# Joining setup, first feed-forward half and RWKV mixing into one block of a two-layer decoder kernel

## What is computed

```python
def rmsnorm(x, g):
    return x * lax.rsqrt(jnp.mean(x * x, axis=-1, keepdims=True) + NORM_EPS) * g

def swiglu(x, w_gate, w_up, w_down):
    return (jax.nn.silu(x @ w_gate) * (x @ w_up)) @ w_down

x = x + 0.5 * swiglu(rmsnorm(x, norm_ffn1[0]), ...)        # D_FF = 2816
# rwkv7_time_mix of h = rmsnorm(x, norm_mix[0]):
xx = jnp.pad(h, ((0, 0), (1, 0), (0, 0)))[:, :-1] - h      # the token before, minus this one
x_r, x_w, x_k, x_v, x_a, x_g = [h + xx * mu[i] for i in range(6)]
r, k, v = x_r @ W_r, x_k @ W_k, x_v @ W_v                  # 1024 x 1024 each
lw = tanh(x_w @ w_lora_a)                                  # 1024 x 64
la = x_a @ a_lora_a                                        # 1024 x 64
lg = sigmoid(x_g @ g_lora_a)                               # 1024 x 160
```

## Time and profile before

| what | value |
|---|---|
| median of three runs | 2573.34 us |
| profiled execution | 2577.01 us |
| its span | 2575.2 us |
| PE busy | 2364.7 us, 92% |
| DVE busy | 1577.5 us, 61% |
| ACT busy | 621.9 us, 24% |
| POOL busy | 576.6 us, 22% |
| mean granted PE clock | 0.96 |
| PE idle before its matmuls of `mix_project` | 28.7 us |

### The profile page before, as it was taken

The page is one execution under the profiler, slowest core; times in us unless marked ns, Lnnn a source line. Parts: engine busy times, 40 slices in busy tenths (PEclk is TensorE's granted clock), DMA queues, the critical chain, the costliest instruction groups (busy, mean ns, idle before and its releaser), DMA issues. The chain is left out here.

```text
span 2575.2 us, 44022 instructions
## 1 busy us (share of the span) xinstructions
PE 2364.7 (92%) x17558; PEld 1920.7 (75%) x17558; DVE 1577.5 (61%) x2151; ACT 621.9 (24%) x1211; POOL 576.6 (22%) x382
## 2 busy tenths in 40 slices
PE   5999995996889869999999999999949998999999
PEld 4888883774666747888888788888738887788887
DVE  5656467982777745656576565657636666565654
ACT  3101012222555432100022310101525552110001
POOL 2202034431222122212130120203221201221211
PEclk8999996998999979999999999999969899999999
DMA  4333321342110022333346233333351102233332
GB/s 119 96 99 98 98 76 54 115 121 84 33 32 26 11 58 86 102 88 102 88 140 184 80 94 95 97 92 103 92 126 38 39 1 66 82 106 90 102 89 71
DMA packets 377090, 217.21 MB, mean 84 GB/s; under 512 B 18881, under 2 KB 360833, under 8 KB 376929
## 3 DMA queue, kind: packets, MB, share of 16 engines
q1 hardware_dynamic: 368800, 199.09, 27.5%
q10 hardware_dynamic: 8128, 15.83, 1.8%
HBM read 199.00 MB, written 15.89 MB: 83 GB/s over the span
## 5 line engine op out<-in xcount | busy, mean ns | idle before, releaser
L150 PE MATMUL bank_b<-hhi_b,w_hi_b 128*128 128x512 f32 x872 | 346.6, 398 | 3.1 <-DVEq L314 3.1
L152 PE MATMUL bank_b<-hhi_b,w_lo_b 128*128 128x512 f32 x872 | 340.9, 391 | 0.0
L151 PE MATMUL bank_b<-hlo_b,w_hi_b 128*128 128x512 f32 x872 | 340.9, 391 | 0.0
L143 DVE TENSOR_TENSOR w_lo_b<-w_raw,w_hi_b 128x1024 fp32r<-128x1024 f32 (+1 forms) x165 | 289.7, 1756 | 5.7
L150 PEld LDWEIGHTS bank_b<-hhi_b,w_hi_b 128*128 128x128 f32 x872 | 164.7, 189 | 40.9 <-DVEq L314 3.8
L151 PEld LDWEIGHTS bank_b<-hlo_b,w_hi_b 128*128 128x128 f32 x872 | 164.7, 189 | 36.7 <-issue 2.9
L152 PEld LDWEIGHTS bank_b<-hhi_b,w_lo_b 128*128 128x128 f32 x872 | 164.6, 189 | 34.6
L446 POOL TENSOR_TENSOR act_b<-gated_b,usc_b 128x512 f32<-128x512 f32 x44 | 63.9, 1452 | 487.9 <-ACT gated_b L423 487.9
L150 PE MATMUL bank_a<-hhi_a,w_hi_a 128*128 128x512 f32 x352 | 138.5, 393 | 17.5 <-DVE w_lo_a L143 11.9
L332 DVE TENSOR_TENSOR gsc_b<-bank_b,rstd_b 128x512 f32<-128x512 f32 x44 | 30.4, 692 | 194.5 <-PE bank_b L152 184.1
L423 ACT ACTIVATE gated_b<-gsc_b 128x512 f32<-128x512 f32 x44 | 27.9, 634 | 494.8 <-DVE gsc_b L332 494.8
(11 more groups left out here) (366 smaller groups left out, 5204.2 us busy)
## 6 DMA issues: line engine op xcount, KB each, us to landing
w_raw<-in_ffn_w_gate_dram SPq DMA_DIRECT2D x88, 512.0 KB, 3.8
w_raw<-in_ffn_w_up_dram SPq DMA_DIRECT2D x88, 512.0 KB, 3.9
w_raw<-in_ffn_w_down_dram SPq DMA_DIRECT2D x64, 512.0 KB, 3.8
w_raw<-in_ffn_w_down_dram SPq DMA_DIRECT2D x32, 384.0 KB, 3.3
w_raw<-in_rw_w_rkv_dram SPq DMA_DIRECT2D x24, 512.0 KB, 4.2
rkv_scratch<-staged_mix ACTq DMA_DIRECT2D x24, 256.0 KB, 2.4
w_raw<-in_kv_w_dram SPq DMA_DIRECT2D x12, 512.0 KB, 4.9
w_raw<-in_rw_w_o_dram SPq DMA_DIRECT2D x8, 512.0 KB, 4.8
```

Source lines behind the costliest of these rows:

```text
L143: nc.vector.tensor_tensor(lo, raw, fp(hi), ALU.subtract).then_inc(s["w_ready"], 1)
L150: nc.tensor.matmul(out, whi, hi, start=first, stop=False)
L151: nc.tensor.matmul(out, whi, lo, start=False, stop=False)
L152: return nc.tensor.matmul(out, wlo, hi, start=False, stop=last)
```

## The change

Setup, the first Ffn and the mixing become one Block with one Region, one weight ring and one set of semaphores.

- **Entry** takes the place of `setup`. PE transposes the vectors first, then x. DVE, not ACT, copies the x tiles from PSUM, two of them ahead of the splits of units 0 and 1, and the other six between the low parts of the Ffn's first norm. Units 2 and 3 are split after the low parts.
- **Mix** takes the place of `mix_project`. A mixed tile is now h(shifted) * mu + h * (1 - mu): ACT makes the second product (`part_tile`), DVE multiplies and adds the first (`mixed_tile`), ACT rounds, and DVE makes the low part (`low_tile`), which POOL did. POOL has nothing to do in Mix. The table 1 - mu (`one_mu`) is made once by DVE.
- The factor of the norm is exp(-0.5 ln(ms)), two ACT operations, in place of ACT's root and DVE's reciprocal.
- The first three r units run side by side, tile by tile; before it was one.
- The mixing's first four units are loaded and split by the ring at the end of the Ffn. On DVE each unit is now: mix and lower the tiles beside it, then split the unit four ahead.
- r and v tiles use the Ffn's `hhi` and `hlo`, k tiles its `ahi` and `alo`; only lw, la and lg use a pair allocated behind `h`. The four slots of unfinished tiles and the two of outputs are in the Ffn's `gsc`, `usc`, `gated` and `act32`.

```diff
@@ class Ffn: vector, scalar, gpsimd @@
-        if self.first:
-            region.split(dve, 0)
-            for d in range(ND):
-                self.norm.vector_tile(dve, d)
-            for u in range(1, 4):
-                region.split(dve, u)
@@ class Mix (new, in place of mix_project) @@
+    def mixed_tile(self, dve, m):
+        d = self.tiles[m][1]
+        dve.wait_ge(self.s["tmp"], m + 1)
+        at = self.core.row["rw_mu"] + self.column(m)
+        self.core.nc.vector.scalar_tensor_tensor(out=self.slot(m), in0=self.h[:, d, 0:T], scalar=self.core.vecs[:, at:at + 1], in1=self.slot(m),
+                                                 op0=ALU.mult, op1=ALU.add).then_inc(self.s["mix32"], 1)
+    def low_tile(self, dve, m):
+        name, d = self.tiles[m]
+        hi, lo = self.pair[name]
+        dve.wait_ge(self.s["mix_hi"], m + 1)
+        self.core.nc.vector.tensor_tensor(lo[:, d], self.slot(m), fp(hi[:, d]), ALU.subtract).then_inc(self.s["mix_lo"], 1)
+    def vector(self, dve):
...
+        self.normal_tile(dve, 0)
+        self.normal_tile(dve, 1)
+        for d in range(ND):
+            self.mixed_tile(dve, d)
+            if d + 2 < ND:
+                self.normal_tile(dve, d + 2)
+            if d:
+                self.low_tile(dve, d - 1)
+        self.low_tile(dve, ND - 1)
+        for u in range(len(self.units)):
+            made = self.made_beside(u)
+            for m in made:
+                self.mixed_tile(dve, m)
+            for m in made:
+                self.low_tile(dve, m)
+            self.region.split(dve, self.base + u + 4)
+    def part_tile(self, act, m):
+        s, (_, d) = self.s, self.tiles[m]
+        act.wait_ge(s["h"], d + 1)
+        if m >= 4:
+            act.wait_ge(s["mix_lo"], m - 3)
+        self.core.nc.scalar.activation(self.slot(m), self.h[:, d, 1:T + 1], ACT.Copy,
+                                       scale=self.one_mu[:, self.column(m):self.column(m) + 1]).then_inc(s["tmp"], 1)
+    def scalar(self, act):
...
+        A(region.ms[:], region.bank[:, 6], ACT.Ln, scale=1.0 / D, bias=self.core.eps[:, 0:1]).then_inc(s["ln"], 1)
+        act.wait_ge(s["ln"], 1)
+        A(region.rstd[:], region.ms[:], ACT.Exp, scale=-0.5).then_inc(s["rstd"], 1)
+        self.part_tile(act, 0)
+        for d in range(ND):
+            if d + 1 < ND:
+                self.part_tile(act, d + 1)
+            self.high_tile(act, d)
+        for u, (name, j) in enumerate(self.units):
+            made = self.made_beside(u)
+            for m in made:
+                self.part_tile(act, m)
+            for m in made:
+                self.high_tile(act, m)
+            act.wait_ge(region.ring["w_free"], done(self.base + u))
...
+    def tensor(self, pe):
+        s, region = self.s, self.region
+        self.norm.tensor_sum(pe)
+        for k in range(ND):
+            pe.wait_ge(s["mix_lo"], k + 1)
+            for u in range(3):
...
+                mm = three_passes(self.core, region.bank[:, u], u, k, hi[:, k], lo[:, k], k == 0, k == ND - 1)
@@ class Entry (new, in place of setup) @@
+    def vector(self, dve, norm):
...
+        residual(0)
+        residual(1)
+        self.region.split(dve, 0)
+        self.region.split(dve, 1)
+        dve.wait_ge(s["vecs"], 2)
+        for d in range(ND):
+            if d + 2 < ND:
+                residual(d + 2)
+            dve.wait_ge(s["copied"], d + 1)
+            norm.vector_tile(dve, d)
+        self.region.split(dve, 2)
+        self.region.split(dve, 3)
+        r = core.row["rw_mu"]
+        V.tensor_scalar(self.one_mu[:], core.vecs[:, r:r + 6 * ND], -1.0, 1.0, ALU.mult, ALU.add)
+    def tensor(self, pe):
...
+        pe.wait_ge(s["rows"], 16 * self.loads)
+        for tile, n in enumerate((P, core.rows - P)):
+            mm = core.nc.tensor.transpose(bank[:, tile, 0:n], self.rows[0:n, tile], core.ident[0:n, 0:n])
+        mm.then_inc(s["rows_turned"], 1)
+        pe.wait_ge(s["x"], 16 * NT)
+        for d in range(ND):
+            if d >= 4:
+                pe.wait_ge(s["copied"], d - 3)
...
@@ opening @@
+        region = Region(core, ctx, tag, early=[sb("tok", [P, NT, D]), sb("rows", [P, 2, P])])
+        h = region.sb("h", [P, ND, T + 1])
+        extra = region.sb("mhi", [P, ND, T], F32R), region.sb("mlo", [P, ND, T], F32R)
...
+            entry.vector(dve, ffn.norm)
             ffn.vector(dve)
+            mix.vector(dve)
```

More of the change, by code:

```diff
@@ L159, with __init__ @@
 class Region:
-    def __init__(self, core, ctx, tag, wide=(), narrow=()):
+    def __init__(self, core, ctx, tag, wide=(), narrow=(), early=()):
         self.core, self.nc, self.ctx, self.tag = core, core.nc, ctx, tag
-        self.owned, self.units = {}, []
+        self.owned, self.units, self.right = {}, [], set()
+        self.early = self.alias(*early)
         self.wide = [self.alias(*rows) for rows in wide]
@@ L197, in take, with cols @@
         return base
+    def cols(self, u):
+        m = self.units[u].shape[2]
+        return slice(P - m, P) if u in self.right else slice(0, m)
     def load(self, sp, u):
         if u >= SLOTS:
-            load_unit(sp, self.ring, self.core, u % SLOTS, u, self.units[u])
+            load_unit(sp, self.ring, self.core, u % SLOTS, u, self.units[u], self.cols(u))
     def split(self, dve, u):
@@ L205, in split @@
             _, k, m = self.units[u].shape
[L206 removed]
+            split_unit(dve, self.ring, self.core, u % SLOTS, u // SLOTS, u, k, m, self.cols(u))
 class Norm:
@@ L411, in scalar @@
         act.sem_inc(s["silu"], 1)
-        if self.first:
-            for d in range(ND):
-                self.norm.scalar_tile(act, d)
         self.norm.scalar_root(act)
@@ L434, in gpsimd @@
         pool.sem_inc(s["a_lo"], 1)
-        if self.first:
-            for d in range(ND):
-                self.norm.pool_tile(pool, d)
         ftile = 0
@@ L1997, in opening @@
+def opening(core, weights, tag, gain, rkv, lora, ahead):
+    with ExitStack() as ctx:
+        sb = lambda name, shape, dt=F32: (f"{name}", shape, dt)
+        region = Region(core, ctx, tag, early=[sb("tok", [P, NT, D]), sb("rows", [P, 2, P])])
+        h = region.sb("h", [P, ND, T + 1])
+        extra = region.sb("mhi", [P, ND, T], F32R), region.sb("mlo", [P, ND, T], F32R)
+        one_mu = region.sb("one_mu", [P, 6 * ND])
         ffn = Ffn(region, f"{tag}_f", *weights)
-        ffn.norm = Norm(region, f"{tag}_n", gain)
@@ L1999, in opening @@
-        ffn.after = Norm(region, f"{tag}_m", None, ffn.x_ready())
+        mix = Mix(region, f"{tag}_x", rkv, lora, h, extra, one_mu)
+        entry = Entry(region, f"{tag}_e", *region.early, one_mu)
+        ffn.norm = Norm(region, f"{tag}_n", gain, (entry.s["copied"], 1))
+        ffn.after = mix.norm = Norm(region, f"{tag}_m", None, ffn.x_ready())
         block = ctx.enter_context(core.nc.Block())
@@ L2004, in _ @@
             pe.sem_inc(region.ring["w_free"], SLOTS)
+            entry.tensor(pe)
             ffn.tensor(pe)
+            mix.tensor(pe)
         @block.sync
         def _(sp):
+            entry.sync(sp)
             ffn.sync(sp)
+            mix.sync(sp)
             sp.wait_ge(region.ring["w_ready"], done(len(region.units) - 1))
@@ L2015, in _ @@
             dve.sem_inc(region.ring["w_ready"], SLOTS)
+            entry.vector(dve, ffn.norm)
             ffn.vector(dve)
+            mix.vector(dve)
         @block.scalar
         def _(act):
+            entry.scalar(act, ffn.norm)
             ffn.scalar(act)
+            mix.scalar(act)
         @block.gpsimd
         def _(pool):
+            entry.gpsimd(pool, ffn.norm)
             ffn.gpsimd(pool)
```

378 lines of the change are left out of this document (148 added, 230 removed).

## The result

The changed kernel takes 2546.06 us in the median of four runs (2543.35 to 2549.94), the kernel before 2574.25 us (2572.14 to 2575.23). The ratio is 0.9893 with a 95% interval from 0.9876 to 0.991: 28 us gained, where 40.4 were forecast. The time lies in the stated range (2520 to 2549), but not in the forecast's own part of it (2524 to 2541). The profiled execution is the fastest of the four, 2543.35 us with a span of 2541.6 us; against the earlier trace rows, whose span is 2575.2 us, it is 33.6 us shorter, more than the 28 of the medians. The time up to the recurrence's first load is 31.3 us shorter (573.80 against 605.13), and I split this one by stages.

A forecast was written before the change was run, and what follows sets the result against it. PE bounds the kernel, busy 92% of the span; time is won where it idles, runs at its lower clock or steps slowly. Entry 8.6 + joint 3.2 + mixing 29.9 - close 1.3 = 40.4 us: 2573.3 to 2532.9; range 2520 to 2549.

The forecast's parts named there:

- Entry: Start of the kernel: units 0 and 1 of the Ffn end at 38.1 us, not 46.7; gain 8.6 us.
- joint: From the Ffn's last matmul to mixing's first: two barriers and the reciprocal go; gain 3.2 us, bounds 1 and 5.
- the close: End of mixing, before the recurrence: one close clears 48 semaphores where mixing's had 21; 1.3 us lost.
- PE makes tiles 0 to 4 of two units meanwhile: Entry: PE makes these matmuls before all squares are summed at 31.0 us, leaving the sum and 18 matmuls, 5.5 us.
- B: Entry gives nothing: copies, low parts and POOL's squares hinder each other, PE waits for all squares; 2541.5 us; chance 0.10.
- A: Mixing: a turn of ACT and DVE takes 7.5 us, longer than PE's unit; 2559 us, half of it 2546; chance 0.14.
- the drain: Joint: a skill rule puts 1.38 us on each table switch, making the gain 1.8 us, not 3.2; left out.
- The new wait ahead of lw: Mixing, after the r units: PE stalls 4.0 us for a low tile, bounds 0 and 8.
- the turn of DVE and ACT: Mixing, r units 3 to 7: the work beside one unit takes 4.75 us, under PE's 5.46.
- D: Mixing: DVE's long forms come from whatever else is active, not from POOL, and stay; 2614 us; chance 0.04.
- What the prediction held against D: DVE operations at 408.12 and 437.17 us are short beside busy ACT and PE with POOL idle.
- The addresses: Mixing: r, k and v leave tiles 32 bytes off the grid; steps of 0.2275 us, not 0.2334; 3.4 us of gain.

The follow-up runs named there:

- e1: Changed kernel with DVE giving PE its first two credits for gate and up banks before the entry's work, not behind it: 2532.25 us, ratio 0.9833.
- e7: Changed kernel with mixing's norm by a root on ACT and a reciprocal on DVE, as before: 2545.29 us in one run.
- e3: Changed kernel with the tiles of the next r unit made one unit earlier in mixing: 2539.29 us.
- e10: Changed kernel with DVE again making difference and multiply-and-add of each mixed tile, and POOL the low parts: 2580.21 us in one run.
- e6: Changed kernel with only the first r unit made tile by tile, the others after it: 2546.54 us in one run.
- e4: Kernel before, with an unused buffer of 32 bytes per partition between h and mhi: 2573.4 us, ratio 0.9995.
- e12: Changed kernel with early credit, sum of squares ahead of tile 7, r tiles one unit earlier, clearing on four engines, mhi and mlo ahead of h: 2514.45 us.
- e11: Changed kernel with the semaphores of every stage cleared by SP, ACT, DVE and POOL, a quarter each, not SP alone: 2533.75 us, ratio 0.9848.

## Why the prediction was right, and where it was wrong

**Entry: wrong, and the whole miss is here.** Forecast +8.6, measured -1.3: 9.9 us, against a whole shortfall of 9.1 at the recurrence's first load (40.4 less 31.3; joint and mixing came out 1.1 better than forecast, the close 0.3 worse) and 12.2 between the medians. The durations were good: vectors landed at 11.0 us (10.0), the last x copy ended at 27.98 (27.9), the squares were summed at 31.84 (31.0). The step that failed is "PE makes tiles 0 to 4 of two units meanwhile". PE's queue has a further wait at this place, for the credit of the gate and up banks, in the code printed above and never named in the prediction. Before, DVE gave that credit as the first thing in `Ffn.vector`, with the low parts and splits behind it. The change moved these into `Entry.vector`, ahead of `Ffn.vector`, and so put the credit behind all of them. The prediction followed the instructions that move and not the increment that stays. e1 shows it by moving this increment alone: 11.8 us. That the time lies in the range is luck: the range reached past 2541 only for rivals B and A. Half of A's cost gives 2546, the measured time, yet no unit of mixing shows the waits that A means. Rival B (2541.5, with medians of 2544.1 and 2546.1 measured) had nearly the size, but its reason is refuted: with the credit given early the same copies, low parts and squares let the second matmul behind the sum start at 33.29 us with 17 more to come, so that units 0 and 1 end at 37.4 us, and 38.1 was forecast.

**Joint: right.** Forecast 3.2, measured 3.6 in the profiled run and 16.2 - 13.55 = 2.7 in its repeat. POOL's last sum beside a weight split took 2.24 us, not 1.65; PE's sum 1.13 or 2.08, for which 2.05 stood, so 2.7 is the gain at a like clock. Ln, table load and Exp are 2.63 us, as taken from the recurrence, and e7 gives the 1.45 us over root and reciprocal. Exp starts at 405.00, 0.02 us after its table load has ended, and that starts 0.01 us after Ln's end: the drain which the Trainium skill ("ScalarE: Activation LUTs", "What ACT_TABLE_LOAD costs") puts at 1.38 us is in none of these rows, and the measurement decides for leaving it out.

**Mixing: right, in size and in its parts.** Forecast 159.5 us, measured 158.8. Three units took 18.0 us (unit 0 was free at 427.35, six matmuls before the end), where 18.4 stood. The new wait ahead of lw was forecast as 4.0 us and is 2.34, with low clock behind it (the prediction's own terms add up to 31.75 us and not to the 31.3 printed, so its wait was 4.45); the turn of DVE and ACT that it comes from is 4.58 us, the distance of DVE's casts at 432.01 and 436.59, where I had 4.75. Those six turns are 1.0 us of the difference. e3 removes the wait. The steps were 0.2267 us in r, k and v and 0.2334 in lw, la and lg, where 0.2275 and 0.2334 stood. The rule of the shared port in the Trainium skill ("SBUF — State Buffer", "Who interferes with whom") is borne out three ways: with POOL silent all of DVE's forms are short; e10 has casts at 1.58 us; and in the entry DVE's copies from PSUM take 0.68 us in the middle of POOL's ten busy us, as the rule says of operations with no second SBUF input. Rivals A and D are out: no wait in mixing but one, no long form. What the prediction held against D was misread, though. At 408.12 us PE and ACT were idle (until 413.04 and 410.42), and at 437.17 PE was idle and POOL at work, from 437.27 to 439.53; DVE's subtraction, which had started 0.10 us earlier, stayed short and POOL's took 2.26 us. It is the changed kernel that refutes D, with short forms throughout beside busy ACT and PE.

**What the prediction over-valued within mixing.** The three units side by side stood as one of its changes with 18.4 us, and no price for doing without was given; e6 puts it at 0.8 us, since what it gains at the start it loses ahead of lw. The addresses were to bring 3.4 us: the steps did get shorter, and e4 shows 0.2334 to 0.2290 from 32 bytes alone. In the kernel before that was worth nothing. In the changed one PE is the bound, and e12 shows 0.7 us for the last four units that lay off; for r, k and v it was not taken back by itself.

**Close: right.** Forecast 1.3 lost, 1.6 measured, and e11 shows it to be the clearing, 0.06 us a semaphore.

## What to carry to other kernels

When code moves past a stage's start, list the semaphore increments that stood there and ask who waits for each; a credit given "first thing" is given last once other work is put in front of it. An idle time that the profile puts to "issue" says only that the profile found no releaser. It was an increment that no operation carries at 35.02 us, and one that DVE's low part carries at 458.21: look in the waiting engine's program for every wait ahead of that instruction. And where a stage is bound by one engine's turn, price the turn and not the operation: two changes that shorten the same turn brought 25.8 and 15.0 us each by itself, and 32.8 together.

## What the runs showed that I had not expected

- Clearing semaphores on one engine costs 0.06 us each and stands between stages; dealt to four engines it gave 10 us over the kernel.
- POOL's addition of 128 x 512, 1.26 us alone, took 2.24 us from 399.54 us on, where a subtraction of DVE had started at 399.44. The subtraction kept its 1.22 us. So POOL can be the one that is slowed.
- Tiles 32 bytes off a multiple of 64 made PE step 0.2334 us in place of 0.2290 (e4). In the changed kernel moving such tiles to a multiple of 64 brought 0.2334 down to 0.2267 (e12); why e4 stays at 0.2290 is open. That tiles lie off is worked out from the size of `h` (16416 bytes a partition); no trace gives addresses.
- Two executions of the same kernel differ in where PE's clock rises after the first product: 3.1 us after it in one (35.02 to 38.14), 5.3 us in the other (34.70 to 39.95). The later rise costs 1.1 us by the sum of squares (8.4 us after the first product in one, 9.4 in the other). Single traces of this kernel can't be compared to better than 1 to 1.5 us in any stage in which PE starts at its low clock.
